# Sparse attention's loop, first token tile: VectorE copies both sets of turned weights in one operation, ScalarE none

## The reference, cut to what matters

```python
s = jnp.einsum('bghqd,bgqnkd->bghqnk', qq, kg) * scale      # selected blocks
p_s = jax.nn.softmax(jnp.where(smask, s, NEG), axis=-1)
o_slc = jnp.einsum('bghqnk,bgqnkd->bghqd', p_s, vg)
s = jnp.einsum('bghqd,bgkd->bghqk', qq, kwb) * scale        # window
p_w = jax.nn.softmax(jnp.where(wmask, s, NEG), axis=-1)
o_win = jnp.einsum('bghqk,bgkd->bghqd', p_w, vwb)
return g[..., 0:1] * o_cmp + g[..., 1:2] * o_slc + g[..., 2:3] * o_win
```

## Time and profile before

| | |
|---|---|
| median of 3 runs | 2199.75 us (2198.06 to 2200.24) |
| the profiled execution | 2200.0 us, span 2198.2 us |
| TensorE busy in the span | 2126.4 us, 97% |
| VectorE busy | 875.7 us, 40% |
| ScalarE busy | 324.3 us, 15% |
| mean granted TensorE clock | 0.994 of full speed |

### The profile page before, as it was taken

How to read it: one execution, slowest core, us unless ns; L and a number is a source line. 1 busy time by engine, 2 the same in 40 slices (tenths; PEclk the granted TensorE clock), 3 DMA queues, 4 the chain that set the end, 5 groups by cost and what they waited for, 6 DMA issues and landing times.

```text
span 2198.2 us, 22003 instructions
## 1 busy us (share of the span) xinstructions
PE 2126.4 (97%) x9011; PEld 1096.2 (50%) x9011; DVE 875.7 (40%) x1665; ACT 324.3 (15%) x728; POOL 45.4 (2%) x60
## 2 busy tenths in 40 slices
PE   7999999999999999999999999999999999998998
PEld 4557776455576774445643333333455533333333
DVE  2337565326475565121523333333665422221122
ACT  1221000214310002101300000000234100000000
POOL 0000000000000000000000000000000000000000
PEclk9999999999999999999999999999999999999999
DMA  9437667523077576323499999999721799999996
GB/s 339 144 137 262 220 238 267 187 79 137 29 254 255 197 285 209 116 77 115 187 423 427 426 426 427 427 426 426 282 88 78 266 426 427 426 426 427 426 427 272
DMA packets 142821, 610.69 MB, mean 278 GB/s; under 512 B 15352, under 2 KB 66232, under 8 KB 117504
## 3 DMA queue, kind: packets, MB, share of 16 engines
q1 hardware_dynamic: 135904, 595.81, 68.6%
q0 software_dynamic: 6720, 13.35, 1.7%
q10 hardware_dynamic: 96, 0.10, 0.0%
HBM read 614.76 MB, written 4.33 MB: 282 GB/s over the span
## 4 chain that ended last, share of the span: by engine, by line
PE 93%; DVE 3%; issue 2%; ACT 2%; DMA 1%; SPq 0%; ACTq 0%; DVEq 0%
PE psum L2207 21%; PE psum L1002 14%; PE psum L515 14%; PE psum L2235 10%; PE psum L2254 8%; PE psum L977 6%; PE psum L1654 4%; PE psum L555 3%; PE psum L2180 1%; PE psum L990 1%; PE psum L628 1%; PE psum L498 1%; PE psum L1804 1%; ACT arena L1431 1%; PE psum L1812 1%
## 5 line engine op out<-in xcount | busy, mean ns | idle before, releaser
L1002 PE MATMUL psum<-normed_t,ring 128*128 128x256 f32 x1408 | 305.5, 379 | 0.0
L1002 PEld LDWEIGHTS psum<-normed_t,ring 128*128 128x128 f32 x1408 | 267.5, 190 | 40.6 <-issue 4.3
L515 PE MATMUL psum<-ring,normed_t 128*128 128x512 f32 x576 | 255.1, 600 | 3.5 <-DMA ring<-in_ab_w_in 1.8
L2207 PE MATMUL psum<-ring,arena 128*64 128x512 f32 x624 | 208.5, 605 | 12.3 <-issue 11.8
L2591 DVE TENSOR_TENSOR resid<-resid,psum 128x512 f32<-128x512 f32 x192 | 131.7, 687 | 186.0 <-PE psum L2254 186.0
L907 DVE SCALAR_TENSOR_TENSOR arena<-ring,silu_c,arena 128x1024 f32<-128x1024 f32 x168 | 204.5, 1277 | 0.0
L515 PEld LDWEIGHTS psum<-ring,normed_t 128*128 128x128 f32 x576 | 109.0, 192 | 134.9 <-issue 132.6
L2599 DVE TENSOR_TENSOR scaled<-scaled,psum 128x512 f32<-128x512 f32 x32 | 22.0, 687 | 303.0 <-PE psum L2207 303.0
L2207 PEld LDWEIGHTS psum<-ring,arena 128*64 128x64 f32 x624 | 67.2, 139 | 125.4 <-issue 125.3
L977 PE MATMUL psum<-ring,arena 128*128 128x512 f32 x288 | 126.3, 596 | 0.0
L2254 PE MATMUL psum<-consts 128*128 128x512 f32 x256 | 115.3, 593 | 0.0
(11 more groups left out here) (440 smaller groups left out, 2672.6 us busy)
## 6 DMA issues: line engine op xcount, KB each, us to landing
ring<-in_w SPq DMA_DIRECT2D x112, 2048.0 KB, 24.5
arena<-in_w SPq DMA_DIRECT2D x44, 2048.0 KB, 26.7
ring<-in_w_mod SPq DMA_DIRECT2D x24, 2048.0 KB, 8.0
ring<-in_ffn_w_up SPq DMA_DIRECT2D x44, 1024.0 KB, 10.1
normed_t<-in_w SPq DMA_DIRECT2D x21, 2048.0 KB, 27.3
consts<-in_w SPq DMA_DIRECT2D x11, 2048.0 KB, 31.9
ring<-in_ffn_w_down SPq DMA_DIRECT2D x10, 2048.0 KB, 9.0
ring<-in_ab_w_in SPq DMA_DIRECT2D x6, 2048.0 KB, 16.0
```

The source lines that it names most:

```text
L515: m = te.eng.matmul(PS[:, bank, 0:n], src[:, k0 + k, P * t:P * t + P], w[:, k, :], start=(k == 0), stop=(k == kc - 1))
L1002: m = pe.matmul(PS[:, b, 256 * hf:256 * hf + 256], w[:, hf, k, P * cc:P * cc + P], HT[:, k, 0:T], start=(k == 0), stop=(k == KC - 1))
L2207: m = pe.matmul(PS[64 * h:64 * h + 64, 2 + q, :], self.XT[c % 2][k // 4][:, k % 4, 64 * h:64 * h + 64], w[h][:, k, :], start=k == 0, stop= ...
```

## The change

A function `turned_by(v, u)` says which engine copies the turned weights of head `u` of pair `v`: VectorE for head 0 always, and for head 1 in the first token tile; ScalarE only for head 1 of the second tile. In the eight passes of tile 0 VectorE copies both banks (`PS[:, 4:6, 0:256]`) into both halves of the `NPT` buffer with one operation, which waits for the turn of head 1 (`nsa.ptr{v}1`) where it waited for that of head 0. Its place in VectorE's stream is unchanged, between the two masks of the next pair. ScalarE's copy in these passes goes. TensorE's waits for bank 5 and for `nsa.pt{v}1` are turned to VectorE's step in these passes. The second tile's passes stay as they were. No transfer is touched.

```diff
--- before.py
+++ after.py
@@ -1351,7 +1351,7 @@
                     t, c = HEADS2[v]
                     for u in range(2):
                         pe.wait_ge(sems["act"], upto("act", f"nsa.e{v}{u}"))
-                        te.take(4 + u, ("dve", "act")[u], f"nsa.pt{v}{u}")
+                        te.take(4 + u, turned_by(v, u), f"nsa.pt{v}{u}")
                         for j in range(2 * (t + 1)):
                             m = pe.transpose(PS[:, 4 + u, P * j:P * j + P], NB[v % 3][:, u, P * j:P * j + P], ident)
                         p.step(m, f"nsa.ptr{v}{u}")
@@ -1371,7 +1371,7 @@
                                                   start=True, stop=True)
                             p.step(m, f"nsa.bcp{gi}{a_}")
                     for u in range(2):
-                        wait(pe, ("dve", "act")[u], f"nsa.pt{v}{u}")
+                        wait(pe, turned_by(v, u), f"nsa.pt{v}{u}")
                     for a_ in range(2):
                         if v % 4 == 0:
                             te.take(6 + a_, "dve", f"nsa.acc{gi}")
@@ -1386,6 +1386,11 @@
                 for n in range(2):
                     rows(te, f"nsa.out{n}", t, 4 + 2 * t + n, ("dve", f"nsa.res{n}{t}"), src=YH, last=t == 1,
                          within={(1, 0): (0, lambda: emb_turn(te, 1)), (1, 1): (0, lambda: norm_pe(te, "n.ffn1", (0,)))}.get((t, n), (-1, None)))
+
+
+
+        def turned_by(v, u):
+            return "dve" if u == 0 or HEADS2[v][0] == 0 else "act"
 
         def nsa_act(ac, p, after):
             def squares(bank, key, cols=512, rows_=P):
@@ -1431,7 +1436,7 @@
                             p.step(ac.activation(NB[w % 3][:, u, o:o + L], NB[w % 3][:, u, o:o + L], ACT.Exp, bias=NMX[:, q:q + 1],
                                                  scale=-1.0, accum_out=NSUM[:, q:q + 1]), *([f"nsa.e{w}{u}"] if a_ else []))
                     v = w - 1
-                    if u == 0 and 0 <= v < n:
+                    if u == 0 and 0 <= v < n and turned_by(v, 1) == "act":
                         L = P * (HEADS2[v][0] + 1)
                         ac.wait_ge(sems["pe"], upto("pe", f"nsa.ptr{v}1"))
                         if v >= 2:
@@ -1593,10 +1598,14 @@
                     v = w - 1
                     if u == 0 and 0 <= v < n:
                         L = P * (HEADS2[v][0] + 1)
-                        dv.wait_ge(sems["pe"], upto("pe", f"nsa.ptr{v}0"))
+                        both = turned_by(v, 1) == "dve"
+                        dv.wait_ge(sems["pe"], upto("pe", f"nsa.ptr{v}{int(both)}"))
                         if v >= 2:
                             dv.wait_ge(sems["pe"], upto("pe", f"nsa.pv{v - 2}"))
-                        p.step(dv.tensor_copy(NPT[v % 2][:, 0, 0:2 * L], PS[:, 4, 0:2 * L]), f"nsa.pt{v}0")
+                        if both:
+                            p.step(dv.tensor_copy(NPT[v % 2][:, :, 0:2 * L], PS[:, 4:6, 0:2 * L]), f"nsa.pt{v}0", f"nsa.pt{v}1")
+                        else:
+                            p.step(dv.tensor_copy(NPT[v % 2][:, 0, 0:2 * L], PS[:, 4, 0:2 * L]), f"nsa.pt{v}0")
                 if w == 1:
                     key_copy(1)
                 v = w - 1
```

## The result

The changed kernel takes 2203.61 us (median of 15 runs, 2201.09 to 2209.62), the kernel before 2199.75 us beside it (15 runs, 2197.09 to 2201.86). The ratio is 1.002, 95% interval 1.0013 to 1.0027: 3.9 us slower, 0.18%. Fifteen runs tell it from nothing, finer than the 0.2% that I had allowed for, and it lies inside these 0.2%. A second set of runs gave 2203.40 against 2200.22 us, ratio 1.0024 (1.0014 to 1.0035).

What follows compares the result with a forecast made beforehand. First-tile passes were held to be set almost evenly by TensorE and ScalarE, then by a 2.53 us ring of waits; 2.45 + 0.32 = +2.8 us gives 2202.6 us beside the median, range 2199.6 to 2205.0.

Steps and rivals of the forecast that it cites:

- the likeliest case: Whole kernel: slower by less than the 0.2% (4.4 us) a measurement can tell; forecast +2.8 us is 0.13%.
- The ring: First-tile passes: turn, copy, next mask and exponentials wait on each other in a circle, 2.53 us a pass, 0.43 more.
- The first term: Passes 1 to 5 of the first tile: pass 5's last pair of exponentials starts 2.45 us later.
- The second term: Passage from first to second tile: the later, longer copy 7 delays the next pass's exponentials, +0.32 us.
- The cover: Pass 7: two second-tile score products at half clock, over 2 us, hide the late exponentials, saving 0.43 us.
- copy 7 waits for the turn at 541.74: Pass 7: the copy starts 0.48 us after that second turn, at 542.22, where it started at 542.16.
- the fall at the group's end: TensorE's clock at half level near 539, after the first four-pair group; if spared +1.4, a second one +4.2 us.
- dear copy: First-tile VectorE copy costing as much as two small ones, 0.68 us instead of 0.60; adds 0.4 us.
- the rival at 13%: Passes 1 to 5: TensorE's clock falls, +1.4 us per pass covered; clearly slower, +5.6 us, 2205.4 us; 13%.
- The rule on sharing: Emptying PSUM: ScalarE and VectorE should both be used; by that alone a loss of 1.6 us.
- Faster: First-tile passes: ScalarE alone sets the pace, eight copies taken off it return 2.1 us, 2197.7 us; 4%.
- Absorbed: After the loop: later transfers from 1080 on take up the 2.8 us loss, result 2199.75 us; 11%.

Runs made afterwards that it cites:

- filled version: The changed kernel plus idle TensorE products in passes 2 to 5 and 7 to keep the clock up; 2201.22 us against 2200.22 before, ratio 1.0011.
- before, filled: The kernel before plus idle TensorE products in pass 7 only; 2198.97 us against 2200.22 before, ratio 0.9997.
- copy last: The changed kernel with VectorE's first-tile copy of both banks placed behind both masks of the next pair; 2199.94 us against 2200.36 before, ratio 1.0000.
- two copies: The changed kernel with two 256-column VectorE copies, one between the masks, one behind both; 2201.11 us against 2200.36 before, ratio 1.0002.

## Why the prediction was right

**The forecast** was +2.8 us, 2202.6; measured +3.9 and +3.2 in two sets, 2203.61 and 2203.40. A slowing within 0.2%, the likeliest case, came true, and the mechanism is the one given. The sum itself is on the low side: +2.8 us is a ratio of 1.0013, at the lower end of both intervals. In the loop, where the loss can be read more finely, it is 3.28 and 3.36 us.

**The ring.** Four links of 0.48, 0.60, 0.54 and 0.91 us were to give 2.53 us a pass. Measured: 2.55 at full clock, in both the changed kernel and its filled version. TensorE, at 1.96 us of work a pass, did not bind. The price of the new copy, 0.60 from start to next, was right: its duration is 0.69 in all eight, as that of the old 512-column form, so reading two banks cost nothing extra here.

**The first term** was +2.45. At full clock it is 14.92 - 12.40 = 2.52.

**The second term** was +0.32, for a seam that lies under half clock as in the kernel before. In the two profiles of the changed kernel, which had a fall there too, it was smaller: the loop lost 3.28 and 3.36 us, pair 5 3.17 and 3.24, so the seam is 0.11 and 0.12. The cover held, and the copy of pair 7 came 0.03 later than pair 5's shift alone, against 0.06 in the prediction; but the 0.26 us by which it holds the queue longer, which the sum took as lost, were mostly made up again: the mask behind it came 0.29 later than that shift (at 546.07), and the mask of the next pair 0.10 (at 547.16). At full clock the term is 2.89 - 2.52 = 0.37, close to the forecast size but by another way. I had let pass 7 lie under two score products at half clock, where the ring costs nothing. In the filled kernel that cover is gone and the ring makes one more turn: the copies of pairs 6 and 7 start at 540.89 and 543.45, 2.56 us apart. Against before, filled, the copy of pair 7 is then 2.73 us late, 0.21 more than pair 5, and the mask behind it 3.00, as its own 0.26 says. The step "copy 7 waits for the turn at 541.74" gave a smaller wait than this, and the slack of 0.1 that followed, before the second tile's passes, was not in it.

**The clock.** The sum had the fall at the group's end alone. One more fall inside passes 1 to 5 was priced at +1.4, which the range took in as +4.2; two such passes, or one with a dear copy, were the rival at 13%. The clock did fall inside, once, at 524, in both profiles of the changed kernel, and its price there was 15.56 - 14.92 = 0.64 us (0.71 in the second). So the sum lacked 0.6 us that came, and the price of such a fall was set at more than twice what it was; +2.8 came as near as it did partly because the seam, 0.2 too dear, stood against the fall left out. In such a pass TensorE's work is stretched, and these are its rows in the changed kernel, beside the 0.66 and 0.70 of the earlier trace rows:

```profile
524.61 1.05 PE L1381 MATMUL psum<-arena 128*64 128x128 f32 x8
525.60 1.23 PE L1347 MATMUL psum<-arena 64*128 64x256 f32 x4
526.75 1.11 PE L1356 MATMUL psum<-consts,arena 128*128 128x128 f32 x4
527.80 0.81 PE L1381 MATMUL psum<-arena 128*64 128x128 f32 x8
```

Between these two weighted sums TensorE has no gap, so in this one pass it, and not the ring, sets the time: 3.19 us, where the ring gives 2.55. I had put 3.9 for 1.96 us of work at half clock; it was 3.19, a stretch of 1.23 us, of which the pass's slack of 0.59 swallowed about half. The argument against a fall, that TensorE would be busy 77% of a pass, was no protection. It was also an average: from 521 to 524, ahead of the fall, TensorE was busy 1.85 of 3 us, and 2.30 of 3 in the kernel before. The page that I cited, TensorE: Matmul & The Clock Gate of the Trainium skill, in its section on psum-queue depth-cycling, says that small idle gaps between groups can make the clock oscillate; the trace agrees, with granted 0.50 at 525 in a stretch without a single gap over 0.9 us, and in the one profile of the changed kernel with its gaps filled the clock stayed up.

The fall at the group's end cost 1.50 us before and 61.99 - 60.10 - 0.64 = 1.25 in the changed kernel. So the loop's 3.28 us are the ring and the seam 2.89, the new fall 0.64, and the old fall 0.25 cheaper; this last is the seam again, 0.11 under the fall against 0.37 at full clock.

**The rule on sharing.** TensorEngine Tiling (Array Packing), section PSUM Bottleneck, of the Trainium skill would have both engines empty PSUM. By that alone I had estimated a loss of 1.6 us, from this case's rows. The runs do not bear it out here as a matter of engines: with both copies on VectorE and no wait for the second turn in front of the mask the loss is nothing (copy last, two copies).

**Faster** at 4% fell: ScalarE's 2.1 us were free to be taken, and at most 0.6 came back (two copies). **Absorbed** at 11% fell too. The chain that ended last has every piece from 577 to 1058 us the same 3.39 us later. First before, then changed:

```profile
614.12 41.44 PE psum L1002 x192
...
1008.64 41.47 PE psum L515 x96
...
1082.13 7.38 PE psum L2191 x64
```

```profile
617.52 41.44 PE psum L1002 x192
...
1012.03 41.47 PE psum L515 x96
...
1085.53 10.15 PE psum L2200 x64
```

**From 3.39 to 4.8 us.** 3.39 us are the loop's 3.28 and 0.11 from ahead of it. The rest of the single profile's 4.8 is chance of the clock elsewhere. The last row of each fence shows it: the same 64 products take 7.38 us before and 10.15 in the changed kernel, where the clock had fallen to 0.50 (rows below), +2.8 us. Near 1730 the kernel before had a fall that the changed one had not, and 1.6 us come back: 3.39 + 2.8 - 1.6 = 4.6, and the last 0.2 are spread over the rest. Not every fall counts in the end: the changed kernel has one more at 1422, yet the two profiles are 6.2 us apart ahead of it and 6.3 at 1521; those of the kernel before at 2012, 2044 and 2104 leave the 4.8 us between them as they were, too.

```profile
1086.00:1088.00 2.00, 2.00 (x20) 2.00 (x19) 0.00 (x0) 1.86 (x2) 0.00 (x0) 1.00 0.99 379
```

```profile
1086.00:1088.00 2.00, 2.00 (x11) 2.00 (x11) 0.96 (x3) 0.00 (x0) 0.00 (x0) 0.50 0.96 408
```

## What to carry to other kernels

Before moving a wait, look at what stands behind it on the same engine and follow that round: here the operation behind the copy fed the very transposes that the copy of the next pass waited for, and a ring of four short links, each read from the trace of before, gave the new pass time to 0.02 us. An operation may double in length at little cost where nobody urgent is queued behind it; a later wait ahead of such a neighbour costs, and length behind that wait costs again, more than the two alone. To merge two copies, place the merged one behind the urgent work, and do not count the relief of an engine that did not set the pass.

## What was not expected of the hardware

The clock of TensorE fell from its upper to its lower level in a loop where TensorE was waiting often but never long (gaps of 0.24 to 0.83 us at 523 and 524), and in the kernel before, with gaps of 0.2 to 0.4 us in the same passes, it did not. Ten small idle products in pass 7 went with an upper clock at the group's end in all five kernels that had them, one profile each; of the seven profiles without them, two of the changed kernel among them, five had the fall there.

The same code with the same gaps falls in one execution and not in another: the transposes and products at 1080 to 1090 ran at full clock in the profile of before and in the second one of the changed kernel, at 0.50 in the first. A single profile's span can so be 1 to 3 us off the next one's; compare stretches, and take the whole time from many runs. What decides which of two alike gaps brings a fall was not tried.
